# Expert stages of a fused transformer kernel: the scatter of a pair's rows moved between the next pair's gate and up products

## The chip, the cores and the metric

The kernel runs on one core of one Trainium2 chip. The metric is the time of one execution on the device, in microseconds; the kernel before took 1945.55 us (median of three runs, 1944.3 to 1945.7). Everything is computed in f32. PE is TensorE, DVE is VectorE, ACT is ScalarE, SP is the engine that issues the loads.

## The reference, cut to what matters

Two blocks of two layers each run one after the other over 256 tokens with 1024 features. The change lies in the second block, whose two layers each end in a mixture of 32 experts; each token goes to two of them:

```python
def expert_block(args):
    xblk, e = args
    hid = jax.nn.silu(xblk @ w_gate[e]) * (xblk @ w_up[e])   # 1024 -> 512
    return hid @ w_down[e]                                    # 512 -> 1024
...
return jnp.zeros_like(h).at[row_tok].add(yb * row_w[:, None])
```

All 32 experts' weights are read in each layer: 6 MB an expert, 201 MB a layer.

## The kernel before, in words

Experts are taken two at a time, 16 pairs (0 to 15) in each of two layers; `experts(0)` and `experts(1)` are the two stages. Each expert has a fixed capacity of 64 token rows, so a pair fills the 128 partitions. For a pair, PE does these steps, each with 128 x 128 weights unless said otherwise:

- **gate** and **up** (`product_of`, whose matmuls are recorded at L1143 of `gate_step`): 8 k-steps for each of two experts, of 512 columns, with the tokens (128 x 64) as weights. The two experts' halves go to the two halves of the array's columns. 32 recorded matmuls each; the products go to PSUM banks 0 and 1.
- **turn of the weights** (`turn_weights`, L1211): two transposes that turn the pair's token weights (tile `weigh`) into bank 2; DVE copies them to `spread` (L2296).
- **scatter** (`scatter`, `add_rows`, L1131): 8 matmuls, recorded as 16, of 256 columns, that add the rows `yt` of the pair *before*, weighted by `spread`, into accumulators in banks 4 to 7. So a scatter must come before DVE overwrites `spread` for the next pair.
- **turn of the hidden rows** (`turn_hidden`, L1223): four transposes of `hs`, which DVE makes (L2289, L2292) from ACT's sigmoid and the two products. DVE copies the result to `hg` (L2298).
- **gather** (`gather`, L1125): the *next* pair's tokens, two halves of 16 recorded matmuls; ACT copies them out to `xg`.
- **down** (`down`, L1241): 32 recorded matmuls with `hg` (128 x 64) as weights; ACT copies the rows to `yt`.

The order on PE inside the loop over pairs 1 to 14 is: gate, up, turn of the weights, scatter, turn of the hidden rows, gather (both halves), down. Pair 0 stands ahead of the loop: gate, turn of the weights, up, first half of the gather, turn of the hidden rows, second half, down. Pair 15 stands behind it, with no gather and its scatter in two halves around the turn of the hidden rows.

On DVE the loop's order is `eg` (L2289), `hs` (L2292), the eight mask operations for the next pair (`masks`, L2276 and L2267), the copy of `spread`, the copy of `hg`. ACT does the sigmoid, the copies of the gathered tokens, the two halves of `yt`.

The order of all engines is written out by hand, with semaphores. The weights go through a ring with room for exactly one pair: three parts, gate, up and down, of 4 MB each. SP issues the next pair's load of a part when the product that reads that part is done (`load_pair`, L1343): gate when gate is done, up when up is done, down when down is done. All loads go through one queue in that order.

Of the kernel before, what the change touches and what calls it, by code (L numbers as in the profile page):

```python
# [17 lines left out]
ALU = mybir.AluOpType  # L18
# [5 lines left out]
KT = D // P  # L24
T = 256
# [97 lines left out]
def build(nc, a, out):  # L123
    with ExitStack() as ctx:
# [35 lines left out]
        ps = ctx.enter_context(nc.psum_tensor("ps", [P, 8, 512], F32))  # L160
# [81 lines left out]
        turned = region(8704, 2, 4 * T)  # L242
# [27 lines left out]
        hg = region(3584, HTL * PAIR)  # L270
        sg = region(4096, EH)
        eg = region(4608, EH)
        pick = region(5120, TT, PAIR)
        weigh = region(5376, TT, PAIR)
        spread = region(5632, T)
# [139 lines left out]
        def _(pe):  # L415
# [171 lines left out]
            n, w = next_chunk()  # L587
# [6 lines left out]
            n, w = next_chunk()  # L594
# [9 lines left out]
            n, _ = next_chunk(TAPS_SLOT)  # L604
            pe.wait_ge(glu_spread, 16 * GROUPS * GROUPS)
            for j in range(HTL):
                b = next_bank()
                for r in range(ROUNDS):
                    last = four_groups(b, j, lambda n: conf_taps[:, ROUNDS * n + r, :],
                                       lambda n: rep_glu[:, n, GROUPS * r:GROUPS * r + T], r == 0, r == ROUNDS - 1)  # L610
# [4 lines left out]
            for j in range(HTL):  # L615
                turn.take(S["tiles_convolved"])
                last = mm(ps[:, b, 0:T], ones[:], cv[:, j, :], start=(j == 0), stop=(j == HTL - 1))
# [131 lines left out]
            for k in range(KT):  # L749
                at = QUAD * (k % GROUPS)  # L750
                last = mm(ps[at:at + QUAD, b, 0:T], gw[:, k, :], h[:, k, :], start=(k < GROUPS), stop=(k >= KT - GROUPS),
                          skip_group_check=True)
# [9 lines left out]
            n, w = next_chunk()  # L762
# [3 lines left out]
            for g in range(2):  # L766
                last = mm(ps[0:8, b, g * T:(g + 1) * T], cst("gate_fold")[:, 8 * g:8 * g + 8], gate_sums, start=True, stop=True)
# [3 lines left out]
            n, w = next_chunk()  # L771
# [4 lines left out]
            for t in range(TT):  # L776
                last = nc.tensor.transpose(ps[:, b, 8 * t:8 * t + 8], ghead[:, 0, t * P:(t + 1) * P],
                                           ident[0:8, 0:8])
# [76 lines left out]
            n, w = next_chunk()  # L855
# [60 lines left out]
            n, w = next_chunk()  # L916
# [72 lines left out]
            for i in range(2 * HTL):  # L989
# [8 lines left out]
                else:  # L998
                    norm_transposes()
                    spatial_gate(2)  # L1000
                    last = spatial_gate(3)
# [183 lines left out]
            def gathered_tokens(e_, first):  # L1185

                last_pair = NEXP // 2 - 1
                pair_of = [matrices(first, e) for e in range(2)]
                arrived, loads, _ = pair_of[0]

                def pair_arrived(j, i, after=0):

                    pe.wait_ge(arrived[j], 16 * i + loads[j] + after)

                def product_of(j, i, from_k, full):
                    for k in range(from_k, KT):
                        if j == 0 and k == KT // 2:
                            pe.wait_ge(e_["xg_ready"], 2 * i + 2)
                        last = gate_step(k, [pair_of[e][2][j] for e in range(2)], j)
                    last.then_inc(full, 1)  # L1200

                def gate_and_up(i, yt_before):
                    for j, full in enumerate((e_["gate_full"], e_["up_full"])):
                        pe.wait_ge(e_["xg_ready"], 2 * i + 1)
                        pe.wait_ge(e_["yt_ready"], yt_before + j)
                        pair_arrived(j, i, 16 * (j == 0))
                        product_of(j, i, 0, full)

                def turn_weights():
                    for t in range(TT):  # L1210
                        last = nc.tensor.transpose(ps[:, 2, t * P:(t + 1) * P], weigh[:, t, :], ident)  # L1211
                    last.then_inc(e_["weights_turned"], 1)

                def scatter(m0=0, m1=KT):
                    for m in range(m0, m1):
                        last = add_rows(m)
                    if m1 == KT:
                        last.then_inc(e_["scattered"], 1)

                def turn_hidden(i):  # L1220
                    pe.wait_ge(e_["hid_ready"], i + 1)
                    for m in range(HTL):
                        last = nc.tensor.transpose(ps[:, 0, m * P:(m + 1) * P], hs[:, m * P:(m + 1) * P], ident)  # L1223
                    last.then_inc(e_["hid_turned"], 1)

                def gather_next(i, early_rows=False):
                    pe.wait_ge(e_["masks_ready"], i + 3)
                    gather(e_, 0)
                    if early_rows:
                        turn_hidden(i)  # L1230
                    pe.wait_ge(e_["spread_ready"], i + 1)
                    gather(e_, 1)

                def down(i):
                    pe.wait_ge(e_["hg_ready"], i + 1)
                    pe.wait_ge(arrived[2], 16 * i + loads[2])
                    for c in range(2):
                        for k in range(HTL):
                            for e in range(2):
                                at = k * PAIR + e * CAP  # L1240
                                last = mm(ps[e * CAP:(e + 1) * CAP, c, :], hg[:, at:at + CAP],  # L1241
                                          pair_of[e][2][2][:, k, c * 512:(c + 1) * 512],
                                          start=(k == 0), stop=(k == HTL - 1))
                        last.then_inc(e_["down_done" if c else "half_done"], 1)

                product_of(0, 0, KT // 2, e_["gate_full"])
                pe.wait_ge(e_["masks_ready"], 2)
                turn_weights()
                pair_arrived(1, 0)
                product_of(1, 0, 0, e_["up_full"])  # L1250
                gather_next(0, early_rows=True)
                down(0)
                with pe.Fori(0, last_pair - 1) as n:
                    gate_and_up(n + 1, 2 * n + 1)
                    turn_weights()
                    scatter()
                    turn_hidden(n + 1)
                    gather_next(n + 1)
                    down(n + 1)
                gate_and_up(last_pair, 2 * last_pair - 1)  # L1260
                turn_weights()
                scatter(0, KT // 2)
                turn_hidden(last_pair)
                scatter(KT // 2, KT)
                down(last_pair)

            experts(0)
# [540 lines left out]
        def _(dve):  # L1808
# [471 lines left out]
            def masks(e_, pair):  # L2280

                weigh_masks(pair)
                pick_masks(pair).then_inc(e_["masks_ready"], 1)

            def gathered_tokens(e_):

                def hidden_rows(i):
                    dve.wait_ge(e_["gate_sig"], i + 1)
                    V.tensor_tensor(eg, ps[:, 0, :], sg, ALU.mult).then_inc(e_["gated"], 1)  # L2289
                    dve.wait_ge(e_["gated"], i + 1)  # L2290
                    dve.wait_ge(e_["up_full"], i + 1)
                    V.tensor_tensor(hs, ps[:, 1, :], eg, ALU.mult).then_inc(e_["hid_ready"], 1)  # L2292
                    dve.wait_ge(e_["weights_turned"], i + 1)

                def turned(i):
                    V.tensor_copy(spread, ps[:, 2, 0:T]).then_inc(e_["spread_ready"], 1)  # L2296
                    dve.wait_ge(e_["hid_turned"], i + 1)
                    V.tensor_copy(hg, ps[:, 0, :]).then_inc(e_["hg_ready"], 1)  # L2298

                last_pair = NEXP // 2 - 1  # L2300
                dve.wait_ge(e_["gate_sig"], 1)
                V.tensor_tensor(eg, ps[:, 0, :], sg, ALU.mult).then_inc(e_["gated"], 1)
                dve.wait_ge(e_["weights_turned"], 1)
                V.tensor_copy(spread, ps[:, 2, 0:T]).then_inc(e_["spread_ready"], 1)
                masks(e_, 1)
                dve.wait_ge(e_["gated"], 1)
                dve.wait_ge(e_["up_full"], 1)
                V.tensor_tensor(hs, ps[:, 1, :], eg, ALU.mult).then_inc(e_["hid_ready"], 1)
                dve.wait_ge(e_["hid_turned"], 1)
                V.tensor_copy(hg, ps[:, 0, :]).then_inc(e_["hg_ready"], 1)  # L2310
                with dve.Fori(0, last_pair - 1) as n:
                    hidden_rows(n + 1)
                    masks(e_, n + 2)
                    dve.wait_ge(e_["scattered"], n + 1)
                    turned(n + 1)
                hidden_rows(last_pair)
                dve.wait_ge(e_["hid_turned"], last_pair + 1)
                V.tensor_copy(hg, ps[:, 0, :]).then_inc(e_["hg_ready"], 1)
                dve.wait_ge(e_["scattered"], last_pair)
                V.tensor_copy(spread, ps[:, 2, 0:T]).then_inc(e_["spread_ready"], 1)  # L2320

            def experts(l):
# [224 lines left out]
```

## Time and profile before

| | |
|---|---|
| median of the runs | 1945.55 us |
| the profiled execution | 1944.3 us, span 1944.3 us |
| PE busy | 1912.8 us, 98% of the span |
| DVE, ACT busy | 586.9 us, 425.4 us |
| the load queue | 588.70 MB in 38626 packets |
| chain of work that ended last, by engine | PE 75%, DMA 22%, DVE 2%, ACT 1% |
| its largest pieces | L472 27%, loads of `in_w_up` 21%, L1143 16% |
| the two loops over pairs 1 to 14 | 907 to 1312 us and 1498 to 1904 us |

The chain is followed back from the last instruction; a piece marked DMA is time in which the next step waited for a load. Timeline rows give the start and the time of a group of equal instructions, and in brackets how long the engine was idle before it and what ended that.

### The profile page before, as it was taken

To read this page: it belongs to the slowest core of one execution; us is meant where nothing else is said; L and a number is where in the kernel's file an instruction comes from. 1 tells how busy PE (TensorE), PEld (TensorE's weight loads), DVE (VectorE), ACT (ScalarE), POOL (GpSimd) and SP (SyncE) were. 2 spreads that over 40 slices of the span, in tenths; PEclk is the share of its full clock that TensorE was granted. 3 is DMA by queue.
4 is the path that set the end of the run, shared out by engine and by line. 5 is a ranking of instruction groups with operands and counts; after the bars stand their busy time and mean duration, and the time that the engine had idled before them with its cause. 6 is when DMAs were issued, how large, how long until landed. Compare 5 with 4: busy or idle time off the path is not lost.

```text
span 1944.3 us, 24445 instructions
## 1 busy us (share of the span) xinstructions
PE 1912.8 (98%) x10126; PEld 1279.5 (66%) x10126; DVE 586.9 (30%) x1356; ACT 425.4 (22%) x952; POOL 12.6 (1%) x27
## 2 busy tenths in 40 slices
PE   8999999999999999999999999999999999999998
PEld 7798888857988888674454454456875544544544
DVE  3279550432755504532111111113222111111112
ACT  3440000322301003422221211213013112212212
POOL 1000000000001000000000000000000000000000
PEclk9999999999999999999999999999999999999999
DMA  9746675522477751238999999999328999999995
GB/s 298 263 174 278 275 306 202 224 91 87 162 293 303 315 198 50 88 141 335 425 432 432 432 431 431 431 431 421 146 87 323 422 433 431 433 433 432 431 431 222
DMA packets 39274, 591.82 MB, mean 304 GB/s; under 512 B 5010, under 2 KB 13466, under 8 KB 15138
## 3 DMA queue, kind: packets, MB, share of 16 engines
q1 hardware_dynamic: 38626, 588.70, 73.6%
q10 hardware_dynamic: 576, 2.10, 0.3%
q8 instruction: 53, 0.87, 0.2%
q14 instruction: 19, 0.16, 0.0%
HBM read 585.31 MB, written 1.05 MB: 302 GB/s over the span
## 4 chain that ended last, share of the span: by engine, by line
PE 75%; DMA 22%; DVE 2%; ACT 1%; issue 0%; DVEq 0%; SPq 0%
PE ps L472 27%; DMA ring<-in_w_up 21%; PE ps L1143 16%; PE ps L713 8%; PE ps L1241 5%; PE ps L1125 3%; PE ps L1131 2%; PE ps L542 2%; PE ps L759 2%; PE ps L631 1%; PE ps L574 1%; PE ps L920 1%; PE ps L1278 1%; PE ps L960 1%; PE ps L527 1%
## 5 line engine op out<-in xcount | busy, mean ns | idle before, releaser
L1143 PE MATMUL ps<-ring,work 128*64 128x512 f32 x2048 | 450.1, 593 | 6.9 <-DMA ring<-in_w_up 6.7
L472 PE MATMUL ps<-h,ring 128*128 128x256 f32 x2048 | 447.3, 380 | 0.8 <-DVE h L1880 0.8
L472 PEld LDWEIGHTS ps<-h,ring 128*128 128x128 f32 x2048 | 387.8, 190 | 59.5 <-issue 7.0
L1143 PEld LDWEIGHTS ps<-ring,work 128*64 128x64 f32 x2048 | 149.4, 137 | 299.6 <-issue 287.3
L1465 ACT ACTIVATE work<-ps 128x512 f32<-128x512 f32 (+2 forms) x183 | 93.9, 521 | 722.4 <-PE ps L472 325.0
L1241 PE MATMUL ps<-ring,work 128*64 128x512 f32 x1024 | 226.8, 595 | 0.0
L1465 ACT ACTIVATE work<-ps,ada,scale_g 128x128 f32<-128x128 f32 x256 | 96.4, 457 | 390.3 <-PE ps L1125 390.3
L2289 DVE TENSOR_TENSOR work<-ps,work 128x512 f32<-128x512 f32 x30 | 20.7, 692 | 518.6 <-ACT work L1465 518.6
L1241 PEld LDWEIGHTS ps<-ring,work 128*64 128x64 f32 x1024 | 70.6, 137 | 132.2 <-issue 128.6
L713 PE MATMUL ps<-work,ring 128*128 128x256 f32 (+1 forms) x704 | 148.6, 373 | 0.0
L1825 DVE SCALAR_TENSOR_TENSOR work<-ring,silu_c,work 128x512 f32<-128x512 f32 x196 | 143.7, 754 | 5.1
L713 PEld LDWEIGHTS ps<-work,ring 128*128 128x128 f32 x704 | 130.5, 190 | 18.7 <-issue 1.7
L1125 PE MATMUL ps<-work 128*128 128x128 f32 x1024 | 121.6, 277 | 2.1 <-DVE work L2267 2.1
L1125 PEld LDWEIGHTS ps<-work 128*128 128x128 f32 x1024 | 118.4, 194 | 3.9 <-issue 3.9
L1131 PE MATMUL ps<-work 128*128 128x256 f32 x512 | 116.3, 380 | 0.0
L1131 PEld LDWEIGHTS ps<-work 128*128 128x128 f32 x512 | 94.6, 190 | 13.1 <-issue 1.6
L1465 ACT ACT_TABLE_LOAD x65 | 83.4, 1283 | 7.6 <-DMA ring<-in_ab_w_in 6.5
L472 PE MATMUL ps<-work,ring 128*128 128x256 f32 x352 | 80.7, 388 | 1.7 <-DVE work L2383 1.4
L472 PEld LDWEIGHTS ps<-work,ring 128*128 128x128 f32 x352 | 67.2, 193 | 15.1 <-issue 3.6
L2292 DVE TENSOR_TENSOR work<-ps,work 128x512 f32<-128x512 f32 x30 | 20.7, 692 | 179.6 <-PE ps L1143 179.6
L1835 DVE TENSOR_TENSOR tmp<-tmp,sq 128x128 f32<-128x128 f32 (+1 forms) x74 | 24.1, 328 | 99.4 <-ACT sq L1465 98.7
L1465 ACT ACTIVATE sq<-x 128x256 f32<-128x256 f32 (+1 forms) x96 | 33.2, 352 | 61.5 <-DVE x L1825 55.1
(301 smaller groups left out, 1189.7 us busy)
## 6 DMA issues: line engine op xcount, KB each, us to landing
ring<-in_w_up SPq DMA_DIRECT2D x32, 4096.0 KB, 21.9
ring<-in_w_down SPq DMA_DIRECT2D x32, 4096.0 KB, 16.7
ring<-in_w_gate SPq DMA_DIRECT2D x30, 4096.0 KB, 19.4
ring<-in_w_ada SPq DMA_DIRECT2D x24, 2048.0 KB, 8.8
ring<-in_w_ff_gate SPq DMA_DIRECT2D x10, 2048.0 KB, 13.5
ring<-in_w_ff_up SPq DMA_DIRECT2D x10, 2048.0 KB, 13.6
ring<-in_w_ff_down SPq DMA_DIRECT2D x8, 2048.0 KB, 13.5
ring<-in_ml_w_in SPq DMA_DIRECT2D x6, 2048.0 KB, 10.4
```

The source lines that it names most:

```text
L472: last = mm(ps[:, b, 0:T], w[:, k, m * P:(m + 1) * P], rhs[:, k, :], start=(i == 0), stop=(i == nk - 1))
L542: last = mm(ps[:, banks[m], half(t)], w[:, k, m * P:(m + 1) * P], u[:, k, half(t)], start=(k == 0), stop=(k == KT - 1))
L713: last = mm(ps[:, banks[m], 0:cols.stop], w[:, k - k0, m * P:(m + 1) * P], ff[:, k, cols], start=(k == 0), stop=(k == FT - 1))
L759: last = mm(ps[:, b, :], h[:, k, t * P:(t + 1) * P], w[:, k, :], start=(k == 0), stop=(k == KT - 1))
L1125: last = mm(ps[:, 3 - half, k * PAIR:(k + 1) * PAIR], htok[:, t, (4 * half + k) * P:(4 * half + k + 1) * P], pick[:, t, :], start=(t == 0) ...
L1131: return mm(ps[:, 4 + m // 2, (m % 2) * T:(m % 2 + 1) * T], yt[:, m * P:(m + 1) * P], spread, start=False, stop=False, skip_group_check=True)
L1143: last = mm(ps[e * CAP:(e + 1) * CAP, j, :], xg[:, k, e * CAP:(e + 1) * CAP], w[e][:, k, :], start=(k == 0), stop=(k == last_k), skip_grou ...
L1241: last = mm(ps[e * CAP:(e + 1) * CAP, c, :], hg[:, at:at + CAP], pair_of[e][2][2][:, k, c * 512:(c + 1) * 512], start=(k == 0), stop=(k == ...
L1465: return nc.scalar.activation(out_, in_, f, bias=bias, scale=scale, **kw)
L1825: return V.scalar_tensor_tensor(out=out_, in0=in0, scalar=scalar, in1=in1, op0=op0, op1=op1)
L1835: step(V.tensor_tensor(ssum[:, s], sq[:, 0, s] if k == 1 else ssum[:, s], sq[:, k, s], ALU.add), S["summed"] if k == KT - 1 else vchain)
L2289: V.tensor_tensor(eg, ps[:, 0, :], sg, ALU.mult).then_inc(e_["gated"], 1)
```

## The change

In pairs 1 to 14 PE's order becomes: gate, scatter, turn of the weights, up, first half of the gather, turn of the hidden rows, second half, down. In pair 15 it becomes: gate, scatter, up, turn of the weights, turn of the hidden rows, down. Pair 0 is as it was. DVE's order in the loop becomes `eg`, `spread`, masks, `hs`, `hg`. No instruction is added or taken away, and the conditions of the loads are the same.

```diff
                 def gate_and_up(i, yt_before):
-                    for j, full in enumerate((e_["gate_full"], e_["up_full"])):
-                        pe.wait_ge(e_["xg_ready"], 2 * i + 1)
-                        pe.wait_ge(e_["yt_ready"], yt_before + j)
-                        pair_arrived(j, i, 16 * (j == 0))
-                        product_of(j, i, 0, full)
+                    pe.wait_ge(e_["xg_ready"], 2 * i + 1)
+                    pe.wait_ge(e_["yt_ready"], yt_before)
+                    pair_arrived(0, i, 16)
+                    product_of(0, i, 0, e_["gate_full"])
+                    pe.wait_ge(e_["yt_ready"], yt_before + 1)
+                    pe.wait_ge(e_["spread_ready"], i)
+                    scatter()
+                    if isinstance(i, int):
+                        pair_arrived(1, i)
+                        product_of(1, i, 0, e_["up_full"])
+                        turn_weights()
+                        return
+                    turn_weights()
+                    pair_arrived(1, i)
+                    product_of(1, i, 0, e_["up_full"])
...
                 with pe.Fori(0, last_pair - 1) as n:
                     gate_and_up(n + 1, 2 * n + 1)
-                    turn_weights()
-                    scatter()
-                    turn_hidden(n + 1)
-                    gather_next(n + 1)
+                    gather_next(n + 1, early_rows=True)
                     down(n + 1)
                 gate_and_up(last_pair, 2 * last_pair - 1)
-                turn_weights()
-                scatter(0, KT // 2)
                 turn_hidden(last_pair)
-                scatter(KT // 2, KT)
                 down(last_pair)
...
-                def hidden_rows(i):
+                def spread_rows_out(i):
                     dve.wait_ge(e_["gate_sig"], i + 1)
                     V.tensor_tensor(eg, ps[:, 0, :], sg, ALU.mult).then_inc(e_["gated"], 1)
+                    dve.wait_ge(e_["scattered"], i)
+                    dve.wait_ge(e_["weights_turned"], i + 1)
+                    V.tensor_copy(spread, ps[:, 2, 0:T]).then_inc(e_["spread_ready"], 1)
+
+                def hidden_rows(i):
                     dve.wait_ge(e_["gated"], i + 1)
                     dve.wait_ge(e_["up_full"], i + 1)
                     V.tensor_tensor(hs, ps[:, 1, :], eg, ALU.mult).then_inc(e_["hid_ready"], 1)
-                    dve.wait_ge(e_["weights_turned"], i + 1)
-
-                def turned(i):
-                    V.tensor_copy(spread, ps[:, 2, 0:T]).then_inc(e_["spread_ready"], 1)
                     dve.wait_ge(e_["hid_turned"], i + 1)
                     V.tensor_copy(hg, ps[:, 0, :]).then_inc(e_["hg_ready"], 1)
...
                 with dve.Fori(0, last_pair - 1) as n:
+                    spread_rows_out(n + 1)
+                    masks(e_, n + 2)
                     hidden_rows(n + 1)
-                    masks(e_, n + 2)
-                    dve.wait_ge(e_["scattered"], n + 1)
-                    turned(n + 1)
```

## Rows read from the trace of the kernel before

**Rows 1.** Chain of waits in order of time: start, time, what

```profile
1064.61 21.89 DMA ring<-in_w_up
1086.64 7.10 PE ps L1143 x32
1093.76 21.88 DMA ring<-in_w_up
```

**Rows 2.** Timeline of PE and its weight loads, pair 1 of layer 0

```profile
907.40 13.90 PE L1143 MATMUL ps<-ring,work 128*64 128x512 f32 x64
...
921.23 0.20 PEld L1211 LDWEIGHTS ps<-con,work 128*128 128x128 f32 x2 [0.81 <-issue]
...
921.50 3.62 PE L1131 MATMUL ps<-work 128*128 128x256 f32 x16
...
924.96 0.60 PE L1223 MATMUL ps<-con,work 128*128 128x128 f32 x4
...
929.06 1.08 PE L1241 MATMUL ps<-ring,work 128*64 128x512 f32 x4
...
935.98 1.03 PE L1143 MATMUL ps<-ring,work 128*64 128x512 f32 x4
```

**Rows 3.** Timeline of PE, pair 0 of layer 0

```profile
888.89 0.44 PE L1211 MATMUL ps<-con,work 128*128 128x128 f32 x2
...
889.26 7.09 PE L1143 MATMUL ps<-ring,work 128*64 128x512 f32 x32
...
896.27 2.05 PE L1125 MATMUL ps<-work 128*128 128x128 f32 x16
...
900.48 7.09 PE L1241 MATMUL ps<-ring,work 128*64 128x512 f32 x32
```

**Rows 4.** Timeline of pair 15 of layer 0, PE, its weight loads and DVE

```profile
1312.37 7.04 PE L1143 MATMUL ps<-ring,work 128*64 128x512 f32 x32
...
1319.74 7.09 PE L1143 MATMUL ps<-ring,work 128*64 128x512 f32 x32 [0.33 <-DMA ring<-in_w_up]
...
1326.93 0.69 DVE L2292 TENSOR_TENSOR work<-ps,work 128x512 f32<-128x512 f32 x1 [6.16 <-PE ps L1143]
...
1328.54 0.57 PEld L1223 LDWEIGHTS ps<-con,work 128*128 128x128 f32 x4
...
1329.46 0.69 DVE L2318 COPY work<-ps 128x512 f32<-128x512 f32 x1 [1.84 <-PE ps L1223]
1331.02 0.20 PEld L1241 LDWEIGHTS ps<-ring,work 128*64 128x64 f32 x4 [0.33 <-issue]
```

**Rows 5.** Timeline of PE in layer 1: gate of pair 1, then pair 15

```profile
1498.41 1.89 PE L1143 MATMUL ps<-ring,work 128*64 128x512 f32 x8
...
1903.59 7.04 PE L1143 MATMUL ps<-ring,work 128*64 128x512 f32 x32
...
1911.31 7.09 PE L1143 MATMUL ps<-ring,work 128*64 128x512 f32 x32 [0.68 <-DMA ring<-in_w_up]
...
1922.59 7.09 PE L1241 MATMUL ps<-ring,work 128*64 128x512 f32 x32
```

**Rows 6.** Groups by line and shape, 907 to 1312 us, DVE's masks

```profile
L2276 DVE TENSOR_SCALAR work<-con,work 128x64 f32<-128x64 f32 x56 | 13.6, 306 | 0.0
```

**Rows 7.** Loads by tile: start of issue and landing, layer 0, gate of pair 2

```profile
L1343 SPq DMA_DIRECT2D ring<-in_w_gate x1: 362/362/362, 914.6 to 914.6; - x1
...
DMA to landing us min/median/max: 15.9/15.9/15.9
```

**Rows 8.** Layer 1, the first load of down in the loop

```profile
L1343 SPq DMA_DIRECT2D ring<-in_w_down x1: 327/327/327, 1498.6 to 1498.6; - x1
...
DMA to landing us min/median/max: 13.9/13.9/13.9
```

**Rows 9.** Layer 0, the load of gate for pair 15

```profile
L1343 SPq DMA_DIRECT2D ring<-in_w_gate x1: 333/333/333, 1290.4 to 1290.4; - x1
...
DMA to landing us min/median/max: 19.5/19.5/19.5
```

More of the change, by code:

```diff
@@ L1212, in turn_weights, with scatter @@
                     last.then_inc(e_["weights_turned"], 1)
-                def scatter(m0=0, m1=KT):
-                    for m in range(m0, m1):
+                def scatter():
+                    for m in range(KT):
                         last = add_rows(m)
-                    if m1 == KT:
-                        last.then_inc(e_["scattered"], 1)
+                    last.then_inc(e_["scattered"], 1)
                 def turn_hidden(i):
@@ L2311, in gathered_tokens @@
                 with dve.Fori(0, last_pair - 1) as n:
+                    spread_rows_out(n + 1)
+                    masks(e_, n + 2)
                     hidden_rows(n + 1)
-                    masks(e_, n + 2)
-                    dve.wait_ge(e_["scattered"], n + 1)
-                    turned(n + 1)
+                dve.wait_ge(e_["gate_sig"], last_pair + 1)
+                V.tensor_tensor(eg, ps[:, 0, :], sg, ALU.mult).then_inc(e_["gated"], 1)
                 hidden_rows(last_pair)
-                dve.wait_ge(e_["hid_turned"], last_pair + 1)
-                V.tensor_copy(hg, ps[:, 0, :]).then_inc(e_["hg_ready"], 1)
                 dve.wait_ge(e_["scattered"], last_pair)
+                dve.wait_ge(e_["weights_turned"], last_pair + 1)
                 V.tensor_copy(spread, ps[:, 2, 0:T]).then_inc(e_["spread_ready"], 1)
```

## The prediction

> **What bounds the kernel now.** I read the chain of waits first. From pair 7 of layer 0 (pair 6 of layer 1) on, each pair has a piece of DMA, the load of up, and these pieces start 29.15 us apart [rows 1]. Three parts of 4 MB in 29.15 us are 9.72 us a part: there the load queue sets the pace. Then I read the timeline of an early pair, where no load is waited for: the gate product starts at 907.40 and the next one at 935.98, so a pair costs PE 28.58 us [rows 2]. PE is thus the faster by 0.57 us a pair, but with nothing to spare early on: it eats up a lead over the loads, and then waits for up in every pair. Both regimes together give the loop of 14 pairs from gate of pair 1 to gate of pair 15: 1312.37 - 907.40 = 404.97 us in layer 0 [rows 2, 4], 1903.59 - 1498.41 = 405.18 us in layer 1 [rows 5]. That is 28.93 and 28.94 us a pair. Whatever the change does to a pair on PE has to be set against 28.93, not against 28.58.
>
> **What the loop costs after the change.** No instruction comes or goes. What changes is how often PE goes from the products with 64-column weights (gate, up, down: narrow) to those with 128-column weights (turns, scatter, gather: wide) and back. Before, a pair does so once each way, since down, gate and up run in one stream. After, gate ends in the scatter, and up stands alone between wide ones: twice each way.
>
> The trace shows what that costs. Ahead of the first wide weight load after up, the weight loads stand idle for 0.81 us [rows 2]: the next weights are not brought in behind the running products. In matmul time:
> - Four transposes and 32 gathers take 929.06 - 924.96 = 4.10 us in the loop, where they follow the scatter [rows 2], and 900.48 - 896.27 = 4.21 us in pair 0, where they follow a narrow product [rows 3]. Beginning after a narrow product costs 0.11 us.
> - The turn of the weights takes 921.50 - 921.23 = 0.27 us when the wide scatter follows [rows 2] and 889.26 - 888.89 = 0.37 us when a narrow product follows [rows 3]. Going back costs 0.10 us.
>
> So I build the new pair from pieces. Down, with gate behind it: 935.98 - 929.06 = 6.92 us [rows 2]. Gate, now the last of its stream: two products in a stream took 921.23 - 907.40 = 13.83 us [rows 2], half is 6.92, and a product that stands alone took 896.27 - 889.26 = 7.01 us [rows 3]; I take 6.97. Scatter 924.96 - 921.50 = 3.46 us [rows 2]. Turn of the weights with both ends 0.37 us [rows 3]; as it is now the scatter that begins after gate, and not the short turn, I add 0.05 of the 0.11. Up alone 7.01 us, gather, turn of the hidden rows and gather 4.21 us, both as in pair 0 [rows 3]. Sum: 6.92 + 6.97 + 3.46 + 0.42 + 7.01 + 4.21 = 28.99 us, 0.41 more than before. The unknown is this added change of shape, and pair 0 is the nearest row. Its bounds are zero (28.58: a matmul stream with no seams; nothing in a reordering of the same instructions goes below) and, from above, the whole idle time of 0.81 us for each of two new changes (30.2), of which pair 0 shows only a fifth.
>
> A page of the Trainium skill speaks against this change too: TensorEngine Tiling (Array Packing), Key Properties, says that changing the tiling mode, not just the tile, drains the TensorE. The price is on another page, TensorE: Matmul & The Clock Gate, Single matmul latency, which puts a drain at about 175 ns. Twice that a pair would be an estimate of 0.35 us where the rows give 0.41, and a total 1.7 us lower than mine.
>
> At 28.99 PE is still faster than the queue's 29.15, so no load is waited for in the loop. Check at its end: gate of pair 15 landed at 1290.4 + 19.5 = 1309.9 [rows 9], and PE comes to it at 907.40 + 14 x 28.99 = 1313.26. Up was there at 1319.6, before PE wants it. **The wait for up (in 9 or 10 pairs a layer) goes, and the added seams take its place, nearly to the microsecond**: gate of pair 15 starts 0.89 us later in layer 0 (1313.26 against 1312.37) and at 1498.41 + 405.86 = 1904.27, 0.68 us later, in layer 1 [rows 4, 5].
>
> **Pair 15.** Before, gate to up was 7.37 us in layer 0 and 7.72 in layer 1, with the wait in it [rows 4, 5]. After, gate, scatter and up: 6.97 + 3.46 + 0.11 + 0.10 = 10.64 us. Before, up to down was 1331.02 - 1319.74 = 11.28 us [rows 4], with the scatter covering DVE's work. After, nothing is left to cover it but the turn of the weights (0.37, done while DVE works). The handshake in a row: up to `hs` 1326.93 - 1319.74 = 7.19, `hs` 0.69, the turn of the hidden rows until DVE's copy 1329.46 - 1328.54 = 0.92, the copy 0.69 [rows 4], and twice about 0.05 for the signal: 9.59 us. It saves 1.69 us of the 3.46 us of scatter. Behind down all is as before; the last `spread` copy is done by then.
> - Layer 0: down starts at 1313.26 + 10.64 + 9.59 = 1333.49, against 1331.02: +2.47 us.
> - Layer 1: 1904.27 + 10.64 + 9.59 = 1924.50, against 1922.59 [rows 5]: +1.91 us.
>
> **What I cost at nothing.** Masks: eight operations, 2 x 13.6 / 14 = 1.9 us a pair [rows 6], with the copy of `spread` 0.4 more. They now run behind scatter and turn, beside up (7.01 us), and are due at the first gather; if up did not cover them, it would be up to 2.4 us a pair. `hs` (0.69 and two signals) lies under the first half of the gather, and the copy of `hg` under the second, as in pair 0, where PE did not stop [rows 3]. The load of up goes out 3.9 us later after gate's, past nothing else, as SP issues in the same order; gate's and down's go out as before. For pair 2 the load of up used to go out when up ended (921.2) and gate of pair 2 landed at 914.6 + 15.9 = 930.5 [rows 7]: a lead of 9.3 us becomes 5.4. A load before which the queue was almost empty took 13.9 us [rows 8], of which 9.7 are the transfer: 4.2 us of lead are enough, and the lead grows from pair to pair. If the queue did run empty once or twice, gate would still have landed 5.5 us before its product (930.5 against 935.98), so it would not show.
>
> **Sum.** +2.47 + 1.91 = +4.4 us on the profiled execution's 1944.3, which lies 1.25 below the median. On the median of 1945.55: **1949.9 us**. A measurement of this kernel can tell 0.2%, 3.9 us, from no change. The forecast is just beyond that. Every 0.1 us in the pair is worth 2.8 us.
>
> **Rivals.**
> - *The seams are free and gate becomes the wait.* Then PE stays at 28.58, runs ahead of up, and from about pair 12 (5.5 us of lead at pair 2, less 0.57 a pair) stands waiting for the gate load instead. Gate of pair 15 starts 0.14 us after landing, as up did (1086.64 against 1064.61 + 21.89 [rows 1]), at 1310.1; with 10.43 us to up and 9.59 to down, down starts at 1330.1, 0.9 us earlier than before; in layer 1, where the wait was 0.35 longer, 1.2 earlier. Total -2.1: 1943.4. This is all that can be won, as the load queue never stops. For it: between down, gate and up no seam shows. Against it: the 0.37 and 4.21 us of pair 0. It holds up to a pair of 28.75 us. Chance 0.13.
> - *The seams are dearer in the loop than in pair 0.* The scatter has 128 columns of weights per matmul, against the two small transposes from which I took the change there. If the two new changes cost over 0.57 us a pair together, PE becomes the bound and the loads wait for it. At 0.7 us: 28 x 0.29 = 8.1 us more, 1958.0. Against it: nothing in rows 3 is longer. Chance 0.1.
> - *The seams cost somewhat less or more than I read*, 28.90 to 29.05: +1.9 to +6.1 us, the forecast's own range, 1947.4 to 1951.7. Chance 0.75, of which about 0.42 lies above 3.9 us.
>
> **Numbers.** Slower by over 0.2%: 0.42 + 0.1, rounded down as it stands at the edge: 0.5. Faster by over 0.2% would take more than the loads allow: 0.04. Within: 0.46. The range 1943.8 to 1953.5 leaves out most of the dear seams and the last tenths of the free ones.
>
> **What would show it.** Gate of pair 1 to gate of pair 2 at 28.9 to 29.05 us instead of 28.58; the DMA pieces of up gone from the chain of waits; two idle times of about 0.8 us of the weight loads a pair (before L1131 and before L1125) instead of one; up of pair 15 to its down at 9.6 us; no wait of PE for DVE in the loop. I am wrong if PE waits for gate's load in the last pairs (the first rival), if the pair is above 29.15 (the second), or if PE is idle before L1125 for the masks.

## The result, and the profile after

| | before | after |
|---|---|---|
| median (9 runs each) | 1945.70 us (1943.44 to 1947.46) | 1949.17 us (1947.87 to 1952.23) |
| ratio | | 1.0017, 95% interval 1.0009 to 1.0025 |
| profiled execution's span | 1944.3 us | 1945.8 us |
| down of pair 0 to down of pair 15, layer 0 | 430.54 us | 432.58 us |
| the same, layer 1 | 431.10 us | 432.58 us |

The changed kernel is 0.17% slower: 3.47 us between the medians. The interval leaves out zero, and it holds the edge of 0.2% that the prediction set. The two stages of these two profiles differ by as much: 2.04 + 1.48 = 3.52 us (each is the start of the last group of L1241 less that of the first; after the change down is L1250). That the two numbers agree to 0.05 us is in part luck: the interval allows 1.8 to 4.9 us, and in a second profile of the kernel before the stage of layer 1 was 1.0 us longer than here. The rest of the kernel is the same work, but its length moves by some us from run to run (the down of pair 0 of layer 0 stands between 899.0 and 903.8 us in the fourteen profiles of this study). Here it was 2.0 us shorter after the change, which is why the two spans differ by 1.5 us only.

The timeline of PE after the change, pair 1 of layer 0, against [rows 2]:

```profile
906.14 7.04 PE L1143 MATMUL ps<-ring,work 128*64 128x512 f32 x32
913.11 3.72 PE L1131 MATMUL ps<-work 128*128 128x256 f32 x16
916.67 0.38 PE L1221 MATMUL ps<-con,work 128*128 128x128 f32 x2
916.98 7.09 PE L1143 MATMUL ps<-ring,work 128*64 128x512 f32 x32
924.00 2.05 PE L1125 MATMUL ps<-work 128*128 128x128 f32 x16
...
928.20 7.09 PE L1250 MATMUL ps<-ring,work 128*64 128x512 f32 x32
935.12 7.04 PE L1143 MATMUL ps<-ring,work 128*64 128x512 f32 x32
```

Gate to gate is 28.98 us (28.58 before). All 14 pairs of both layers are 28.97 or 28.98; the 29.13 to 29.15 of the late pairs is gone. Its weight loads and DVE in the same pair:

```profile
913.11 3.32 PEld L1131 LDWEIGHTS ps<-work 128*128 128x128 f32 x16 [0.81 <-issue]
...
924.00 1.86 PEld L1125 LDWEIGHTS ps<-work 128*128 128x128 f32 x16 [0.81 <-issue]
```

```profile
924.18 0.69 DVE L2300 TENSOR_TENSOR work<-ps,work 128x512 f32<-128x512 f32 x1 [4.82 <-PE ps L1143]
```

The weight loads now have two idle times of 0.81 us a pair where there was one. DVE's last masks start at 918.39 and take 0.97 us; then it waits 4.82 us for up, so the masks are well covered. The chain that ended last, by engine:

```profile
PE 96%; DVE 2%; ACT 1%; issue 0%; DMA 0%; DVEq 0%; SPq 0%
```

DMA had 22% of it before. Pair 15 of layer 0, against [rows 4]:

```profile
1311.81 7.04 PE L1143 MATMUL ps<-ring,work 128*64 128x512 f32 x32
...
1322.42 7.09 PE L1143 MATMUL ps<-ring,work 128*64 128x512 f32 x32
...
1330.37 0.66 PE L1232 MATMUL ps<-con,work 128*128 128x128 f32 x4 [0.49 <-DVE work L2300]
...
1331.81 7.09 PE L1250 MATMUL ps<-ring,work 128*64 128x512 f32 x32 [0.78 <-DVE work L2302]
```

Gate to up 10.61 us, with no wait for the load; up to down 9.39 us, with 0.49 and 0.78 us of PE waiting for DVE.

### The profile page after: what moved, and what is told of

Its sections match the earlier page's. It is cut to its first block, busy times and chain, and to the rows that moved or that the text cites. A ratio compares the mean times of both kernels' runs of the same rounds, so it can differ in the third digit from the quotient of the medians.

```text
span 1945.8 us, 24487 instructions
## 1 busy us (share of the span) xinstructions
PE 1919.0 (99%) x10126; PEld 1275.7 (66%) x10126; DVE 586.0 (30%) x1356; ACT 425.0 (22%) x952; POOL 12.5 (1%) x27
## 2 busy tenths in 40 slices
DMA packets 39274, 591.82 MB, mean 304 GB/s; under 512 B 5010, under 2 KB 13466, under 8 KB 15138
## 4 chain that ended last, share of the span: by engine, by line
PE 96%; DVE 2%; ACT 1%; issue 0%; DMA 0%; DVEq 0%; SPq 0%
PE ps L472 27%; PE ps L1143 23%; PE ps L1250 12%; PE ps L713 8%; PE ps L1125 6%; PE ps L1131 6%; PE ps L542 2%; PE ps L759 1%; PE ps L631 1%; PE ps L560 1%; PE ps L574 1%; PE ps L1232 1%; PE ps L920 1%; PE ps L1281 1%; PE ps L960 1%; PE ps L527 1%
## 5 line engine op out<-in xcount | busy, mean ns | idle before, releaser
L1143 PEld LDWEIGHTS ps<-ring,work 128*64 128x64 f32 x2048 | 143.8, 137 | 279.2 <-issue 279.0
L1250 PE MATMUL ps<-ring,work 128*64 128x512 f32 x1024 | 226.8, 595 | 1.6 <-DVE work L2302 1.6
L1250 PEld LDWEIGHTS ps<-ring,work 128*64 128x64 f32 x1024 | 70.6, 137 | 133.6 <-issue 128.0
L1125 PE MATMUL ps<-work 128*128 128x128 f32 x1024 | 127.7, 278 | 2.1 <-DVE work L2270 2.1
## 6 DMA issues: line engine op xcount, KB each, us to landing
ring<-in_w_ff_gate SPq DMA_DIRECT2D x10, 2048.0 KB, 13.6
ring<-in_w_ff_up SPq DMA_DIRECT2D x10, 2048.0 KB, 13.8
ring<-in_ml_w_in SPq DMA_DIRECT2D x6, 2048.0 KB, 10.5
```

What stands on the lines that cost most here:

```text
L1125: last = mm(ps[:, 3 - half, k * PAIR:(k + 1) * PAIR], htok[:, t, (4 * half + k) * P:(4 * half + k + 1) * P], pick[:, t, :], start=(t == 0) ...
L1143: last = mm(ps[e * CAP:(e + 1) * CAP, j, :], xg[:, k, e * CAP:(e + 1) * CAP], w[e][:, k, :], start=(k == 0), stop=(k == last_k), skip_grou ...
```

## The experiments

A stage length below is always down of pair 0 to down of pair 15, layer 0 and layer 1, from one profile. It splits into the 14 pairs of the loop and the last step, down of pair 14 to down of pair 15. The kernels were not all measured on one chip: each ratio is to the kernel before on the same chip, whose median was 1945.70 us for the kernel after, 1946.61 for loop only, last pair only, turn between and three seams, and 1947.09 for the last four rows. So medians are compared here by how far they lie above or below their own before.

| kernel | a pair, early / late | 14 pairs | last step | stage | median, ratio to before (interval) |
|---|---|---|---|---|---|
| before | 28.59 / 29.14 | 404.97, 405.18 | 25.57, 25.92 | 430.54, 431.10 | 1945.70 |
| after | 28.98 / 28.98 | 405.66, 405.66 | 26.92, 26.92 | 432.58, 432.58 | 1949.17, 1.0017 (1.0009 to 1.0025) |
| loop only | 28.98 / 28.98 | 405.66, 405.66 | 26.05, 26.35 | 431.71, 432.01 | 1948.90, 1.0011 (1.0001 to 1.0020) |
| last pair only | 28.59 / 29.14 | 406.35, 405.09 | 27.00, 26.99 | 433.35, 432.08 | 1949.04, 1.0014 (1.0004 to 1.0023) |
| turn between | 28.93 / 29.14 | 405.49, 405.11 | 25.74, 26.72 | 431.23, 431.83 | 1946.87, 1.0006 (0.9996 to 1.0015) |
| three seams | 29.32 / 29.32 | 410.53, 410.54 | 26.93, 26.93 | 437.46, 437.47 | 1960.25, 1.0067 (1.0050 to 1.0084) |
| before, half up | 28.59 / 28.59 (layer 1) | 405.25, 400.22 | 25.58, 25.01 | 430.83, 425.23 | 1939.54, 0.9961 (0.9946 to 0.9977) |
| after, half up | 28.98 / 28.98 | 405.66, 405.66 | 26.93, 26.93 | 432.59, 432.59 | 1950.53, 1.0020 (1.0008 to 1.0031) |
| before, down in parts | 28.59 / 29.15 | 404.97, 404.97 | 25.57, 25.56 | 430.54, 430.53 | 1946.90, 0.9997 (0.9987 to 1.0007) |
| after, down in parts | 28.98 / 28.98 | 405.66, 405.66 | 26.93, 26.92 | 432.59, 432.58 | 1949.86, 1.0017 (1.0007 to 1.0027) |

In the two profiles of before and after, the loop is thus longer by 0.69 + 0.48 = 1.17 us and the last step by 1.35 + 1.00 = 2.35: two thirds of the loss lie in pair 15, which is passed once a layer.

**Half of the change each.** First the changed loop with pair 15 as before:

```diff
-                gate_and_up(last_pair, 2 * last_pair - 1)
-                turn_hidden(last_pair)
+                gate_and_up_in_a_row(last_pair, 2 * last_pair - 1)
+                turn_weights()
+                scatter(0, KT // 2)
+                turn_hidden(last_pair)
+                scatter(KT // 2, KT)
                 down(last_pair)
```

> The loop over pairs 1 to 14 as changed, pair 15 in the order of before (gate, up, turn, half scatter, turn of the hidden rows, half scatter, down). My theory (the seams of the loop pay back the waits for up; what is lost is lost in pair 15): a pair in the loop 28.98 us, gate of pair 1 to down of pair 15 423.8 us in layer 0 (before 423.6, changed 425.7), total within 0.5 us of before, about 1946. Rival (the loop itself is what costs): the total stays at the changed kernel's, about 1949.

The pairs came as expected. The stage of layer 0 was 1.0 us longer than I expected (424.8 us from gate of pair 1 to down of pair 15, 1331.39 less 906.60), since pair 15 waited longer for up:

```profile
1320.11 7.09 PE L1143 MATMUL ps<-ring,work 128*64 128x512 f32 x32 [0.81 <-DMA ring<-in_w_up]
```

I had put PE and that load level; PE stood idle for 0.81 us until it landed. The total is 2.3 us above its before, and its interval settles neither theory. The loop is 0.48 to 0.69 us a layer dearer than in this profile of before, and pair 15's old order gives back 0.87 and 0.57 us of the changed kernel's stage.

Then the other half, the loop of before with pair 15 as changed:

```diff
-                gate_and_up(last_pair, 2 * last_pair - 1)
...
+                product_of(0, last_pair, 0, e_["gate_full"])
+                pe.wait_ge(e_["yt_ready"], 2 * last_pair)
+                scatter()
+                pair_arrived(1, last_pair)
+                product_of(1, last_pair, 0, e_["up_full"])
                 turn_weights()
-                scatter(0, KT // 2)
                 turn_hidden(last_pair)
-                scatter(KT // 2, KT)
                 down(last_pair)
```

> The loop of before, pair 15 as changed. My theory: the loop keeps 28.58 us a pair early on and its waits for up later (404.97 and 405.18 us for 14 pairs), and pair 15 costs 1.35 us more in layer 0 and 1.0 in layer 1, so about 2.4 us over before, 1948. Rival (the loop is what costs): as before, within 0.5 us.

The last step cost 1.43 and 1.07 us more than before, as expected, and the total is 2.4 us over the before of its chip. The loop, identical to that of before, I had expected unchanged; it was 1.4 us longer in layer 0, as the waits for up of 0.33 us began in pair 4 and not in pair 7. So the stage of before is not a fixed length.

**What a seam costs.** Narrow are the products with 64-column weights (gate, up, down), wide the turns, the scatter and the gather; a seam is one change from narrow to wide and back. The kernel of before, with nothing moved but the two small transposes:

```diff
                         product_of(j, i, 0, full)
+                        if j == 0 and between is not None:
+                            between()
...
-                    gate_and_up(n + 1, 2 * n + 1)
-                    turn_weights()
+                    gate_and_up(n + 1, 2 * n + 1, turn_weights)
                     scatter()
```

> The kernel of before with one thing moved in the loop: the turn of the weights (two small transposes) between gate and up; the scatter stays behind up. My theory (any wide instruction between two narrow products costs the seam): early pairs 28.95 us instead of 28.58, the waits for up almost gone, gate of pair 1 to down of pair 15 within 0.5 us of before, total 1946. Rival (it is the scatter between the products, its weights or its waits, that costs): early pairs stay at 28.6 us and the waits for up stay.

```profile
935.01 7.04 PE L1143 MATMUL ps<-ring,work 128*64 128x512 f32 x32
941.98 0.44 PE L1213 MATMUL ps<-con,work 128*128 128x128 f32 x2
942.35 7.09 PE L1143 MATMUL ps<-ring,work 128*64 128x512 f32 x32
...
963.95 7.04 PE L1143 MATMUL ps<-ring,work 128*64 128x512 f32 x32
```

963.95 - 935.01 = 28.94 us: 0.35 us more, without the scatter moved at all. So 0.35 of the 0.39 us come from a wide instruction between two narrow products, and not from the scatter's place. The seams hardly show in the loop: 14 x 0.35 = 4.9 us were added, and the 14 pairs took 0.52 us more and 0.07 less than before, as the waits for up went. The stage came out 0.69 and 0.73 us longer, where I had expected 0.5 at most: in pair 15 PE still waited for up, 0.51 and 1.49 us. The total's interval (0.9996 to 1.0015) includes no change.

In the other direction, one seam more than the change has, by half of the scatter in the middle of gate:

```diff
                         if j == 0 and k == KT // 2:
                             pe.wait_ge(e_["xg_ready"], 2 * i + 2)
+                            if midway is not None:
+                                midway()
...
+                        scatter(0, KT // 2)
...
+                        product_of(0, i, 0, e_["gate_full"], first_half)
+                        scatter(KT // 2, KT)
```

> As changed, but in the loop half of the scatter stands in the middle of gate, so that a pair changes between narrow and wide weights three times each way instead of twice. My theory (0.20 us for a change there and back): 29.18 us a pair, just above the load queue's 29.15, 28 x 0.20 = 5.7 us over the changed kernel, about 1955. Rival (the changed kernel's 0.4 us comes from where the scatter stands, not from the number of changes): 28.98 us a pair, no change.

```profile
940.02 3.60 PE L1143 MATMUL ps<-ring,work 128*64 128x512 f32 x16
943.55 1.99 PE L1131 MATMUL ps<-work 128*128 128x256 f32 x8
...
969.34 3.60 PE L1143 MATMUL ps<-ring,work 128*64 128x512 f32 x16
```

29.32 us a pair. The number of changes counts, as my theory says, but my expectation of 29.18 was too low: the 0.20 us for a change there and back are the prediction's two single prices, 0.11 + 0.10. Its sum of the pair has 0.41 us for the same change (28.99 less 28.58), as it also takes gate, up and the turn longer where they stand alone. Measured are 0.35 (before to turn between), 0.39 (before to after) and 0.35 (after to three seams). At 29.32 PE is slower than the queue, nothing is waited for, and every 0.35 us reaches the total: 28 x 0.35 = 9.8 us in the stages, and the median lies 13.6 us above its before, against 3.5 for the changed kernel.

No run tells whether the seam is the price of the change of shape itself or of bringing in wider weights after narrow ones: every wide instruction here has 128 columns of weights, and every narrow one 64.

**Who sets the pace.** In layer 1, half of each load of up is left out, in both orders:

```diff
+                    if l and w == 1 and not isinstance(pair, int):
...
+                        sp.dma_start(slots[:, :, 0:SLOT // 2], src[:, :, 0:SLOT // 2]).then_inc(arrived, 16)
+                        return
```

> The kernel of before with only half of each load of up in layer 1, pairs 2 to 15 (2 MB instead of 4; the products read what was left there by an earlier pair). My theory (before, the load queue set the pace of the later pairs): layer 1's 14 pairs at 28.58 us each, 400.1 us instead of 405.2, and no wait in pair 15, 5.9 us less in all, about 1939.8. Rival (the waits for up come from the order of PE, not from the queue's rate): 405 us, no change.

> The changed kernel with the same half loads of up in layer 1. My theory (after the change PE alone sets the pace, by its own seams): layer 1's 14 pairs stay at 28.98 us each, 405.7 us, total as the changed kernel, 1949.2 within 0.5. Rival (the loads still hold it, through the gate load or by slowing PE): layer 1 shorter by more than 1 us.

The end of layer 1 in the order of before; down of pair 0 started at 1488.90:

```profile
1896.04 13.90 PE L1143 MATMUL ps<-ring,work 128*64 128x512 f32 x64
...
1914.13 7.09 PE L1241 MATMUL ps<-ring,work 128*64 128x512 f32 x32
```

Gate and up of pair 15 are one stream now, with no wait for a load in it. Both stages came out to a tenth of a microsecond: 431.10 to 425.23 us in the order of before (5.87 less), 432.59 in the changed order (no change). The totals are looser: 7.6 us under its before where I expected 5.9 (the interval allows 4.5 to 10.5), and 3.4 us over its before for the changed order, which is the changed kernel's own 3.5, though 1950.53 lies outside the 1949.2 within 0.5 that I wrote. This pair is the clearest result of the study. The queue held the late pairs of before; in the changed kernel PE alone sets the pace. It also shows what the stage of before could be with loads that never hold it: 425.2 us, of which the changed order gives away 7.4.

**Can the queue be helped?** In layer 1 the queue had nearly run empty ahead of pair 1's load of down (issued 1.6 us before the load ahead of it landed), so I sent that load in two parts:

```diff
-                    for w in (1, 2):
-                        sp.wait_ge(freed[w], 1)
-                        load_pair(w, 1)
+                    sp.wait_ge(freed[1], 1)
+                    load_pair(1, 1)
...
+                    for part, half_freed in enumerate((e_["half_done"], e_["down_done"])):
+                        at = slice(part * 512, (part + 1) * 512)
+                        sp.wait_ge(half_freed, 1)
+                        sp.dma_start(to[:, :, at], src[:, :, at]).then_inc(arrived, 16)
```

> The kernel of before, with the load of down for pair 1 in two parts of 2 MB: the first goes out when the first half of down of pair 0 is done, 3.5 us earlier. In layer 1 the queue ran empty there (the load before landed at 1500.2, this one 12.3 us later instead of 9.7). My theory (later pairs are held by a queue that never stops from there on): the queue is 2.6 us earlier in layer 1, the waits for up 2.6 us less in sum, total 2.6 us less or a little more, about 1943. Rival (the queue's start does not matter, or smaller rows of 2 KB cost as much as they win): no change.

> The changed kernel with the same load of down in two parts. My theory (it waits for no load): no change against the changed kernel, 1949.2 within 0.5, and the loop still 405.7 us. Rival (the loads hold it): as much less as with the kernel of before.

The load in two parts, in the order of before, layer 1, against [rows 8]:

```profile
L1392 SPq DMA_DIRECT2D ring<-in_w_down x2: 541/545/549, 1495.3 to 1498.8; - x2
...
DMA to landing us min/median/max: 11.8/12.8/13.8
```

The changed kernel's stages did not move, as expected; its total lies 2.8 us above its before (1949.86, just outside the 1949.2 within 0.5). In the order of before the stage of layer 1 was 0.57 us shorter and that of layer 0 the same, where I expected 2.6 us in layer 1: a miss. The rows show why. The first part went out 3.4 us earlier and landed at 1507.2, but the second landed at 1498.8 + 13.8 = 1512.5, where the whole load had landed before (1498.6 + 13.9). Nothing was won for the load as a whole: its two parts took the queue 12.4 us behind the load ahead, though the first was there 4.8 us before that one had landed. In layer 0 the whole load had landed 9.7 us behind the load ahead of it, and the two parts took 11.0. That is what the rival said, that smaller rows cost as much as they win, though these runs don't tell the rows from the number of loads. The 0.57 us are hardly the split's either: most of them come from pair 15, where PE waited 0.32 us for up and not 0.68, as that load landed 9.7 us behind its predecessor and not 10.0, a difference that comes up without any split (see below).

When I wrote the next expectation I had misread these rows: I took the 13.8 us as counted from the first part, and the load as landed 3.4 us earlier, with a gap behind it. There was none: gate of pair 2 landed 9.7 us behind the second part, so its issue was not too late.

In the next two kernels every load of pairs 1 to 15 goes out in two parts of 2 MB:

```diff
+                    half_freed = e_["gate_half"], e_["up_freed"], e_["half_done"]
...
                     with sp.Fori(0, NEXP // 2 - 2) as i:
                         for w in range(3):
-                            sp.wait_ge(freed[w], i + 2)
-                            load_pair(w, i + 2)
+                            for part, sem_of in enumerate((half_freed, freed)):
+                                sp.wait_ge(sem_of[w], i + 2)
+                                load_half(w, i + 2, part)
```

> The kernel of before, with every load of pairs 1 to 15 issued in two parts of 2 MB, each as soon as its half of the old weights has been read, so the first part goes out 3.5 us earlier. The one-off load of down in two parts won only 0.6 us because the next load, of gate, was issued too late in its turn; here all are early. My theory (the waits for up in the late pairs are owed to gaps in the queue around pairs 1 and 2): the queue gets 3 to 6 us ahead, the waits start later or never, down of pair 0 to down of pair 15 falls from 430.5 and 431.1 us to 426 to 428 (425.2 is what PE needs without any wait), total 5 to 10 us less than before, 1937 to 1942. Rival (the gaps are the price of a load itself, twice as many loads make twice as many gaps): the same or slower, from 430.5 up.

> The changed kernel with the same loads in two parts. My theory (its pairs are bound by PE and its seams): down of pair 0 to down of pair 15 stays at 432.6 us in both layers, total as changed, 1949. Rival (the loads hold it too): as much less as with the order of before.

Both expectations failed. The kernels took 1988.24 us (ratio 1.0219, 1.0205 to 1.0233) and 1988.57 us (1.0217, 1.0202 to 1.0233) against a before of 1945.01, with stages of 450.5 and 452.9 us in the order of before and 450.7 and 450.3 in the changed one. The DMA line of the order of before, and one wait of the changed order:

```profile
DMA packets 120555, 591.83 MB, mean 297 GB/s; under 512 B 6419, under 2 KB 14875, under 8 KB 77987
```

```profile
1056.61 7.09 PE L1143 MATMUL ps<-ring,work 128*64 128x512 f32 x32 [1.36 <-DMA ring<-in_w_gate]
```

There are three times the packets (39274 before), for the halves cut the rows of each load: the weights moved in packets of 32 KB before, now of 8 and 2 KB. In the late pairs the queue moved 410 GB/s instead of 432, and most pairs took 30.7 us in both orders. The queue's engines show no gaps in that stretch (their busy share is 1.03, against 1.00 before), so it is not that each load brings a gap with it; with smaller packets the same bytes took longer. That the packets' size is the reason, and not the number of loads, is argued: no run kept the rows whole and sent twice the loads. My theory of the gaps was not tested by this, as the queue's rate changed with them. What it does show: with a slower queue the changed order waits for gate, the order of before for up, and their totals are the same within the noise. That is the mechanism of my first rival, and it needs a queue slower than PE's pair.

**How steady the stage of before is.** Two kernels once more, for their profiles only:

> The kernel of before once more, unchanged, for its profile. My theory (its loop is held by the load queue, and the queue's position is set by gaps of chance size at the first loads): down of pair 0 to down of pair 15 may differ from 430.5 and 431.1 us by up to 1.5 us in either layer, and by as much as the load of up for pair 15 lands earlier or later; early pairs stay at 28.58. Rival (the stage is a fixed length): 430.5 and 431.1 within 0.2.

> The kernel with the changed loop and pair 15 in the order of before, once more, for its profile. It measured 431.7 and 432.0 us where I expected 430.8 and 431.3, as up of pair 15 was waited for 0.8 and 1.1 us. If those waits came from late first loads by chance, the waits differ this time and the pairs stay at 28.98; if the order of the changed loop itself makes the queue late, they are 0.8 and 1.1 again.

Before again: 430.65 and 432.14 us, early pairs 28.58. Loop only again: 431.28 and 431.89 us, pairs 28.98, waits for up of pair 15 0.38 and 0.99 us instead of 0.81 and 1.11. In layer 0 the stage goes with the first loads: down of pair 1 landed 20.3 us after down of pair 0 began in both profiles of before, whose loops took 405.0 and 405.1 us, and 21.7 in the last-pair-only kernel, whose loop took 406.4. In layer 1 a second cause showed in both: the last load of up landed 10.0 us behind its predecessor in one profile of before and 11.0 in the other, against 9.7 for the loads around it, so that PE waited 0.68 and then 1.69 us. The same load was late in the changed kernel (11.1 us), where PE came to it only after it had landed, so it cost nothing. The traces have a lead on it: in each of the ten profiles with whole loads of up, one packet of 16 KB of the instruction queue moves while layer 1's last load of up does (at 1905.5 us in the profile of before), and that load landed 9.7 to 11.1 us behind its predecessor; in layer 0 no such packet moves there, and it is 9.7 in all ten. But the same packet goes with a delay of nothing up to 1.4 us, and no run took it away, so what delays these loads stays open. The stage in the changed order, which waits for no load, was 432.58 or 432.59 in all six layers profiled, of three kernels (after, after with half up, after with down in parts).

## Why the prediction was right

Forecast 1949.9 us, +4.4 against before; measured 1949.17, +3.47. The forecast's mechanism held, and the growth was overestimated by 0.9 us. Part of the closeness is luck: the stage of before, which the change is measured against, moved by 1.0 us in layer 1 from one profile to the next.

- **A pair in the loop.** Forecast 28.99, measured 28.98. Piece by piece: gate 6.97 (forecast 6.97), scatter and turn 3.87 (3.88), up 7.02 (7.01), gather, turn, gather 4.20 (4.21), down 6.92 (6.92). What made this work was pair 0, which already had the new order's shape. Turn between and three seams confirm that the cause is the change between narrow and wide weights. The prices that the prediction names for it, 0.11 and 0.10, are only half of it; its sum has 0.41 us, a quarter of the twice 0.81 us of idle weight loads, and not a fifth.
- **The waits for up go, the seams take their place.** Right. The loop got 0.69 and 0.48 us longer (forecast 0.89 and 0.68; 14 times the 0.014 us by which the pair was overestimated).
- **Pair 15.** Forecast +1.58 us in layer 0 (10.64 - 7.37 + 9.59 - 11.28) and, by the same working, +1.23 in layer 1; measured 1.35 and 1.00. This is the larger part of the loss, 2.35 of 3.52 us. The mis-sized term is the handshake from up to down: 9.59 forecast, 9.39 measured. I had taken the turn of the hidden rows as 0.92 us from its first weight load to DVE's copy, from a place where the matmuls waited behind a scatter. With PE idle before it, it took 1331.06 - 1330.37 = 0.69 us.
- **Costed at nothing: masks, `hs`, `hg`.** Right: DVE idle 4.82 us before `hs`, and no wait of PE for DVE in the loop.
- **Costed at nothing: the later load of up.** Right for the time, as the half loads and the parts show: nothing in the changed loop waits for a load. The reason was partly wrong. Up of pair 2 did follow with no gap, but I had not looked at the next load: down of pair 2 went out with a lead of 3.8 us instead of 4.4 (the time from its issue to the landing of the load ahead), and landed 11.2 us behind up instead of 9.9. Whether 4.2 us of lead are enough, as I had said, is not settled: with leads of 4.2 to 4.4 us the early loads of down landed 9.9 to 10.6 us behind the load ahead of them in four of the profiles, but in the kernel with three seams most loads of down in the middle of the loop had such leads and landed 9.7 behind. I had said that if the queue ran empty it would not show, and so it was.
- **The rule on the drain.** Changing tiling mode drains the TensorE (the Trainium skill, TensorEngine Tiling (Array Packing), Key Properties); with the 175 ns of TensorE: Matmul & The Clock Gate, Single matmul latency, the estimate was 0.35 us a pair. The traces agree with the rule in that each change there and back cost time, 0.35, 0.39 and 0.35 us, within 0.04 us of the estimate. They don't show a drain as such. And the 175 ns is what that section gives, beside the time of its columns, for a single bf16 matmul, where these are streams in f32; so the agreement in size may be chance.
- **Rivals.** Free seams fell with the first pair, 28.98 and not 28.58 us. Dearer seams fell too; the kernel with three seams shows what they would have done, as PE became the bound at 29.32. Whether the loss is more than 0.2%, to which I gave 0.5, or less, to which I gave 0.46, these runs don't decide (0.17%, 0.09 to 0.25%).

## What to carry to other kernels

When two resources each take nearly the same time for a loop step (28.58 and 29.15 us here), an early lead can be eaten before the waits begin. Set a change against what the loop costs in sum (28.93), not against the step of either regime: removing a wait wins at most the difference, and any cost of the new order comes off it. Count how often an order changes the shape of the weights, not only how many instructions it has; a pair elsewhere in the same kernel that already has the new order is the best price list. A step that covers a handshake in the last pass of a loop should stay there, even where the loop itself no longer needs it: two thirds of this loss came from two passes of 32.

## What the runs showed that I had not expected

- The stage bound by loads varies from profile to profile, in layer 1 from 431.10 to 432.14 us in the kernel of before, by how late the last load landed, and in layer 0 by 1.4 us with the first loads, while the stage bound by PE repeats within 0.01 us.
- Sending a load in two parts, with shorter rows, cost rate: 432 to 410 GB/s when 2 MB parts took the place of 4 MB loads in the whole loop. One such load alone (down of pair 1) lost time too: its two parts took 12.4 and 11.0 us behind the load ahead, where a whole load in the middle of the loop takes 9.7.
